# Differential attention's steps placed between the tiles of its input projection, modulation folds moved to the norms' waits, and tables for the square root fetched ahead

## The reference, cut to what matters

```python
q_x, k_x, v_x, gu_x, gv_x = jnp.split(hx @ w_in, AB_SPLITS, axis=-1)   # 4096 -> 8 chunks of 512
k_c, v_c = jnp.split(hc @ w_in[:, QK_W:2 * QK_W + V_W], [QK_W], axis=-1)
...
s = jnp.einsum('bqhmd,bkhmd->bhmqk', q, k) * ATTN_SCALE      # 8 heads, m = 2, 512 keys
p = jax.nn.softmax(s, axis=-1)
a = p[:, :, 0] - lam * p[:, :, 1]
o = jnp.einsum('bhqk,bkhe->bqhe', a, v)
...
y_x = jnp.concatenate([a_x, g_x], axis=-1) @ w_out
```

## Time and profile before

| | |
|---|---|
| Median of 3 runs | 2482.37 us (2480.27 to 2483.12) |
| The profiled execution | 2483.58 us; its span 2482.2 us |
| Mean granted TensorE clock | 0.961 of full speed |
| Busy | TensorE 2334.6 us (94%), VectorE 1830.6 (74%), ScalarE 1108.0 (45%), GpSimd 365.8 (15%) |
| 0 to 200 us | first block's attention |
| 190 to 390.7 us | up and down projection; of 245 to 290, TensorE is busy 45.00 |
| 400.4 to 546 us | second block's input projection; of 440 to 546, TensorE is busy 106.00 |
| 546 to 627 us | differential attention; of 571 to 608, TensorE is busy 28.00 |
| 633 to 668 us | output projection |
| 679 to 1541 us | first expert stage |

### The profile page before, as it was taken

One profiled execution on the slowest core, in us unless ns is written; L12 is line 12 of the kernel. 1 busy time (PEld: TensorE's weight loads), 2 busy tenths in 40 slices (PEclk: granted clock), 3 DMA queues, 4 the chain that ended last, 5 costly groups with the idle time before them and its releaser, 6 DMA issues.

```text
span 2482.2 us, 38990 instructions
## 1 busy us (share of the span) xinstructions
PE 2334.6 (94%) x15710; PEld 2059.9 (83%) x15710; DVE 1830.6 (74%) x3241; ACT 1108.0 (45%) x1571; POOL 365.8 (15%) x157
## 2 busy tenths in 40 slices
PE   7989998997899999999999997889999999999997
PEld 6769986774689999998777776779999999777785
DVE  8568988737538877778888876846986777888655
ACT  4446534325444444444444443444444444444443
POOL 0000004630434440000000000623440000000000
PEclk9779999998899999999999998989999999999998
DMA  8326674330245555555557884444555555556663
GB/s 295 122 85 210 205 292 176 125 105 1 94 170 179 180 178 165 168 171 170 170 170 276 306 331 172 165 163 157 171 182 166 166 167 169 171 171 218 222 213 118
DMA packets 123202, 442.58 MB, mean 178 GB/s; under 512 B 13696, under 2 KB 16768, under 8 KB 122256
## 3 DMA queue, kind: packets, MB, share of 16 engines
q1 hardware_dynamic: 117288, 425.04, 50.2%
q10 hardware_dynamic: 5736, 15.06, 1.8%
HBM read 436.88 MB, written 3.16 MB: 177 GB/s over the span
## 4 chain that ended last, share of the span: by engine, by line
PE 82%; DVE 13%; ACT 3%; issue 2%; DMA 0%; POOL 0%; ACTq 0%; SPq 0%; DVEq 0%
PE ps L377 25%; PE ps L378 25%; PE ps L379 25%; PE ps L2294 3%; DVE spl L2099 2%; DVE hT L1434 2%; ACT spl L934 1%; DVE acc L1454 1%; DVE hT L1432 1%; PE ps L406 1%; DVE xr L1950 1%; DVE xr L1955 1%; PE ps L2242 1%; ACT ex L1249 1%; DVE ex L1865 0%
## 5 line engine op out<-in xcount | busy, mean ns | idle before, releaser
L2099 DVE TENSOR_TENSOR spl<-ring,spl 128x1024 fp32r<-128x1024 f32 x561 | 691.0, 1233 | 400.6 <-ACT spl L934 399.3
L934 ACT ACTIVATE spl<-ring 128x1024 fp32r<-128x1024 f32 x703 | 738.2, 1052 | 497.2 <-PE ps L379 477.2
L377 PE MATMUL ps<-hT,spl 128*128 128x256 f32 x2656 | 765.4, 288 | 10.5 <-DVE spl L2099 8.5
L378 PE MATMUL ps<-hT,spl 128*128 128x256 f32 x2656 | 756.8, 285 | 0.0
L379 PE MATMUL ps<-hT,spl 128*128 128x256 f32 x2656 | 756.5, 285 | 0.0
L377 PEld LDWEIGHTS ps<-hT,spl 128*128 128x128 f32 x2656 | 515.1, 194 | 15.1 <-DVE spl L2099 9.3
L2355 POOL TENSOR_TENSOR spl<-ring,spl 128x1024 fp32r<-128x1024 f32 x142 | 353.6, 2497 | 1109.4 <-ACT spl L934 1109.3
L378 PEld LDWEIGHTS ps<-hT,spl 128*128 128x128 f32 x2656 | 515.7, 194 | 0.0
L379 PEld LDWEIGHTS ps<-hT,spl 128*128 128x128 f32 x2656 | 515.1, 194 | 0.0
L377 PE MATMUL ps<-spl,Ws 128*128 128x512 f32 x1024 | 414.4, 405 | 10.8 <-DVE Ws L2107 10.6
L378 PE MATMUL ps<-spl,Ws 128*128 128x512 f32 x1024 | 406.9, 397 | 0.0
(11 more groups left out here) (374 smaller groups left out, 2502.6 us busy)
## 6 DMA issues: line engine op xcount, KB each, us to landing
ring<-in_peer_u SPq DMA_DIRECT2D x256, 512.0 KB, 3.5
ring<-in_peer_v SPq DMA_DIRECT2D x256, 512.0 KB, 3.5
vring<-in_ada_w SPq DMA_DIRECT2D x56, 512.0 KB, 6.2
ring<-in_w_up SPq DMA_DIRECT2D x44, 512.0 KB, 4.3
aring<-in_ada_w SPq DMA_DIRECT2D x40, 512.0 KB, 5.5
ring<-in_ab_in SPq DMA_DIRECT2D x32, 512.0 KB, 3.4
ring<-in_peer_wq SPq DMA_DIRECT2D x32, 512.0 KB, 3.9
ring<-in_w_down SPq DMA_DIRECT2D x22, 512.0 KB, 5.3
```

The source lines that it names most:

```text
L377: q.matmul(o, l[0], r[0], start=start, stop=False)
L378: q.matmul(o, l[0], r[1], start=False, stop=False)
L934: q.activation(P.spl[:, m % SPLITS, 0, 0:w], P.ring[:, m % SLOTS, 0:w], ACT.Copy).then_inc(*P.hi.mark(m))
L2099: q.tensor_tensor(P.spl[:, n % SPLITS, 1, 0:w], P.ring[:, n % SLOTS, 0:w], P.spl[:, n % SPLITS, 0, 0:w].bitcast(F32), ALU.subtract).then_i ...
```

## The change

- **Attention between tiles.** The chunks now come in the order 2, 0, 4, 3, 1, 5, 7, 6. The transposes of queries and keys and the steps are called from within the tile loop, on all three engines: steps 0 to 9 behind the ten tiles from chunk 3's first on, steps 10 to 17 behind the eight tiles of chunks 7 and 6, steps 18 and 19 in the output stage. `ab_step(s)` says which head-half is scored, transposed and multiplied in a step. Steps have one pair of score banks and one bank each for transposes and values, no longer two. The rotations, the gate's norm and lambda are likewise called at single tiles.
- **Low halves** of all tiles before the first expert stage are VectorE's (`lo_on_dve`).
- **Context.** Its modulation goes from VectorE in the projection to ScalarE (two passes) and VectorE (one) at every second down tile.
- **Folds.** 0 goes behind the output projection of the first block, 3 and 4 behind the down projection, 9 and 10 behind the first expert stage, each between the last tile and `pe_turns`. The three modulation steps in the first output projection go to the up projection. Folds no longer all wait for the one before, only for one that shares a bank.
- **Up projection.** The cast of the product goes to ScalarE, and the split trails one pair of tiles.
- **Tables.** A one-column square root (`act_ready_sqrt`) at seven places loads the table ahead.
- **Output stage.** The groups come in the order 0, 1, 4, 5, 2, 3 and are copied and split in pairs of 512 columns; four output tiles run before heads 4 to 7 are transposed.

```diff
+AB_CHUNK = (2, 0, 4, 3, 1, 5, 7, 6)
+AB_STEP = {(3 + s // 4, s % 4): s for s in range(10)}
+AB_STEP.update({(6 + s // 4, s % 4): 10 + s for s in range(8)})
+AB_TURN = {(1, 3): ("KTc", 0), (2, 0): ("KT", 0), (2, 2): ("QT", 0), (5, 2): ("KTc", 1), (5, 3): ("KT", 1),
+           (6, 0): ("QT", 1)}
+def ab_step(s):
+    first, s = 8 * (s // 10), s % 10
+    return (first + s if s < 8 else None, first + s - 1 if 1 <= s < 9 else None, first + s - 2 if s >= 2 else None)
...
-    folds = [("ret", 7), ("up", 42), ("dn", 9), ("dn", 17), ("ab", 6)]
-    folds += [("v", 0, places[8 * i + 7][2] + 3) for i in range(5, 11)] + [("v", 1, 84)]
+    folds = [("wo_end",), ("up", 42), ("dn", 9), ("dn_end",), ("dn_end",)]
+    folds += [("v", 0, places[8 * i + 7][2] + 3) for i in range(5, 9)] + [("v_end",), ("v_end",), ("v", 1, 84)]
...
-    return n < T_AB
+    return n < T_PEER[0]
...
+def act_ready_sqrt(q, P, i):
+    q.wait_ge(*P.set_dve.at("eps"))
+    q.activation(P.none[:, i:i + 1], P.eps1[:, 0:1], ACT.Sqrt).then_inc(*P.line("none").mark())
...
 def pe_ab(q, P):
...
-            pe_fold(q, P, ("ab", 4 * i + p))
+            if (i, p) in AB_TURN:
+                pe_diff_turn(q, P, *AB_TURN[i, p])
+            if (i, p) in AB_STEP:
+                pe_diff_step(q, P, AB_STEP[i, p])
...
+def pe_diff_step(q, P, s):
...
+        for m in range(2):
+            if n % 8:
+                q.wait_ge(*act.at(("x", n - 1, m)))
+            q.matmul(P.ps[4 + m][:, :], P.QT[64 * m:64 * m + 64, h, tb * 128:(tb + 1) * 128],
+                     P.KT[64 * m:64 * m + 64, h, :], start=True, stop=True).then_inc(*pe.mark(("s", n, m)))
+    if nt is not None:
+        q.wait_ge(*dve.at(("mixed", nt)))
...
+        for j in range(4):
+            t = q.transpose(P.ps[6][:, j * 128:(j + 1) * 128], P.ex(nt, 0)[:, j * 128:(j + 1) * 128], P.ident[:, :])
...
 def act_ab(q, P):
...
         for p in range(4):
             act_hi(q, P, T_AB + 4 * i + p + 2)
...
+            if (i, p) in AB_STEP:
+                act_diff_step(q, P, AB_STEP[i, p])
...
 def dve_ab(q, P):
...
         for p in range(4):
-            dve_ada(q, P, ("ab", 4 * i + p))
+            if p == 0 and i and AB_BANK[i - 1][1]:
+                evz(i - 1)
+            dve_lo(q, P, T_AB + 4 * i + p + 2)
...
+            if (i, p) in ropes:
+                rope(*ropes[i, p])
...
+            elif i == 7 and p in (0, 2):
+                dve_gate_norm(q, P, p, act, dve)
...
+            if (i, p) in AB_STEP:
+                dve_diff_step(q, P, AB_STEP[i, p])
...
+def dve_diff_step(q, P, s):
...
+        q.wait_ge(*act.at(("x", nt, 1)))
+        q.reciprocal(z, z).then_inc(*dve.mark())
...
+    if n is not None:
+        for m in range(2):
+            q.wait_ge(*pe.at(("s", n, m)))
+            q.tensor_reduce(P.nm[:, 2 * n + m:2 * n + m + 1], P.ps[4 + m][:, :], AX, ALU.max, negate=True).then_inc(
+                *dve.mark(("mx", n, m)))
...
 def dve_pool(q, P):
...
-    dve_folds(q, P, dve, (1, 0), (1, 1))
+    dve_folds(q, P, dve, (1, 0))
+    dve_ada(q, P, ("v_end",))
+    dve_folds(q, P, dve, (1, 1))
```

More of the change, by code:

```diff
@@ L683, in pe_down @@
         pe_fold(q, P, ("dn", k))
-AB_CHUNK = [(i + 6) % 8 for i in range(8)]
+    pe_fold(q, P, ("dn_end",))
 def pe_ab(q, P):
@@ new lines, in pe_abo, with turns, tile @@
+def pe_abo(q, P):
+    bpe, bact, bdve = P.stage("ab")
+    dpe, dact, ddve = P.stage("da")
+    pe, act, dve = P.stage("abo")
+    def turns(g, bank, free):
+        q.wait_ge(*free)
+        for k in (2 * g, 2 * g + 1):
+            for tb in range(2):
+                q.wait_ge(*(ddve.at(("head", tb, k // 4 * 4)) if k < 8 else bdve.at(("gated", tb))))
+                o = k % 2 * 256 + tb * 128
+                t = q.transpose(P.ps[bank][:, o:o + 128], P.MB[:, tb, k * 128:(k + 1) * 128], P.ident[:, :])
+        t.then_inc(*pe.mark(("turn", g)))
+    def tile(c, j):
+        n = T_ABO + 6 * c + j
+        sl = pe_take(q, P, n)
+        for ks in range(2):
+            k = 2 * ABO_TILE[j] + ks
+            if c == 0:
+                q.wait_ge(*dve.at(("lo", k // 2)))
+            for tb in range(2):
+                if k == 0 and tb == 0:
+                    q.wait_ge(*dact.at(("x", 15, c)))
+                elif k == 0:
+                    q.wait_ge(*(ddve.at(("ao", 15)) if c else dact.at(("eT", 15))))
+                t = mm3(q, P.ps[4 + c + 2 * tb][:, :],
+                        cut(both(P.MT), lambda v: v[:, k, tb * 128:(tb + 1) * 128]),
+                        cut(sl, lambda v: v[:, ks * 512:(ks + 1) * 512]), k == 0, k == 7)
+                if ks == 1:
+                    t.then_inc(*pe.mark(("k", c, k, tb), *([("used", n)] if tb else []),
+                                        *([("y", tb, c)] if k == 7 else [])))
@@ L851, in pe_pool @@
+        t.then_inc(*P.line("ab_pe").mark(("gate", tb)))
+    for g in range(2):
+        turns(g, 2 + g, bact.at(("ev", 7, g)))
+    pe_diff_step(q, P, 18)
+    for g in range(2):
+        turns(4 + g, g, bdve.at(("gated", g)))
+    pe_diff_step(q, P, 19)
+    for j in range(4):
+        tile(0, j)
+    for g in range(2):
+        turns(2 + g, 2 + g, act.at(("turn", g)))
+    for j in range(4, 6):
+        tile(0, j)
+    for j in range(6):
+        tile(1, j)
 def pe_pool(q, P):
@@ new lines, in act_ab @@
+            name, hf = AB_TURN.get((i, p), ("KTc", 0))
+            if name != "KTc":
+                dst, b = (P.KT[:, :, 256:512], 6) if name == "KT" else (P.QT, 4)
+                if name == "KT" and hf == 0:
+                    q.wait_ge(*P.ada_pe.at(("fold", ADA_FRONT - 1)))
+                for g in (2 * hf, 2 * hf + 1):
+                    q.wait_ge(*dpe.at((name, g)))
+                    q.activation(dst[:, 2 * g:2 * g + 2, :], P.ps[b + g % 2][:, :].rearrange("p (k t) -> p k t", k=2),
+                                 ACT.Copy).then_inc(*dact.mark((name, g)))
@@ L1314, in act_peer @@
     tmp = P.ln[key][3][:, :].rearrange("p (a n) -> p a n", a=4)
-    q.wait_ge(*before[2].at("folds"))
+    q.wait_ge(*before[2].at(("folds", l, 1)))
     act_turned(q, pe, act, P.ps, tmp, P.adc[:, l, 3, :], P.adc[:, l, 2, :])
@@ new lines, in dve_head_ms, with dve_head_rms @@
+def dve_head_ms(q, P, h0):
+    act, dve = P.stage("da")[1:]
+    w, x = (v.rearrange("p (t h) -> p t h", t=2)[:, :, h0:h0 + 4] for v in (P.hr, P.hs))
+    q.wait_ge(*act.at(("hs", 2 * h0 + 7)))
+    q.tensor_scalar(w, x, 1.0 / 128, LN_EPS, ALU.mult, ALU.add).then_inc(*dve.mark(("hms", h0)))
+def dve_head_rms(q, P, h0):
+    act, dve = P.stage("da")[1:]
+    hr = P.hr.rearrange("p (t h) -> p t h", t=2)[:, :, h0:h0 + 4]
+    q.wait_ge(*act.at(("hsd", h0)))
+    q.reciprocal(hr, hr).then_inc(*dve.mark())
@@ L1931, in dve_abo, with parts @@
 def dve_abo(q, P):
-    bdve = P.stage("ab")[2]
+    bpe, bact, bdve = P.stage("ab")
     pe, act, dve = P.stage("abo")
+    def parts(*groups):
+        for g in groups:
+            x = P.tmpm[:, (0, 1, 4, 5, 2, 3).index(g) % 2, :].rearrange("p (k t) -> p k t", k=2)
+            hi, lo = P.MT[:, 0, 2 * g:2 * g + 2, :], P.MT[:, 1, 2 * g:2 * g + 2, :]
+            q.wait_ge(*act.at(("turn", g)))
+            q.tensor_copy(hi, x).then_inc(*dve.mark())
+            q.wait_ge(*dve.now())
+            q.tensor_tensor(lo, x, hi.bitcast(F32), ALU.subtract).then_inc(*dve.mark(("lo", g)))
+    q.tensor_scalar(P.dg, P.wcol("dng"), 1.0 - LAM_INIT, None, ALU.mult).then_inc(*dve.mark("dg"))
+    for tb in range(2):
+        q.wait_ge(*bpe.at(("gate", tb)))
+        q.wait_ge(*bact.at(("ev", 7, tb)))
+        for g in range(4):
+            q.scalar_tensor_tensor(
+                out=P.MB[:, tb, 1024 + g * 128:1152 + g * 128], in0=P.ps[tb][:, g * 128:(g + 1) * 128],
+                scalar=P.wcol("sgb", g), in1=P.U[:, tb, g * 128:(g + 1) * 128], op0=ALU.add,
+                op1=ALU.mult).then_inc(*bdve.mark(*([("gated", tb)] if g == 3 else [])))
+    dve_diff_step(q, P, 18)
+    parts(0, 1)
+    dve_lo(q, P, T_ABO + 2)
+    parts(4, 5)
+    dve_diff_step(q, P, 19)
+    dve_head_ms(q, P, 4)
+    dve_lo(q, P, T_ABO + 3)
+    dve_head_rms(q, P, 4)
+    dve_lo(q, P, T_ABO + 5)
+    parts(2, 3)
+    for n in range(6, 14):
+        dve_lo(q, P, T_ABO + n)
     dve_folds(q, P, dve, (0, 1))
-    q.tensor_scalar(P.dg, P.wcol("dng"), 1.0 - LAM_INIT, None, ALU.mult).then_inc(*dve.mark("dg"))
-    for k in range(12):
-        q.wait_ge(*act.at(("turn", k)))
-        hilo(q, dve, P.MT, k, P.tmpm[:, k // 2 % 2, k % 2 * 256:k % 2 * 256 + 256], ("lo", k))
     dve_ln(q, P, "abo", pe, act, dve)
@@ L2215, in pe_peer @@
     if l == 0:
-        first = [b4act.at(("turn", k)) for k in (9, 11, 5, 7)]
+        first = [b4act.at(("turn", g)) for g in (4, 5, 2, 3)]
     else:
@@ L2324, in pe_program @@
     pe_ab(q, P)
-    pe_diff(q, P)
     pe_abo(q, P)
```

641 lines of the change are left out of this document (297 added, 344 removed).

## The result

The changed kernel takes 2459.55 us (median of four runs, 2458.06 to 2464.22), the kernel before beside it 2481.32 (2477.16 to 2483.12): a ratio of 0.9918, 95% interval 0.9899 to 0.9937. The profiled run of the changed kernel took 2458.46, its span is 2456.8 against 2482.2. The forecast was 2457 between 2438 and 2476. The total is right; a sum of terms can be right by luck, so the stretches are compared one by one.

A forecast was written before the change was run, and what follows sets the result against it. TensorE, with 82% of the chain, was taken to bound the kernel. Gains of 4.0, 2.4, 1.9, 6.5 and 11 make 25.8 us; 2483.6 less that and 1.2 for the median gives 2457, range 2438 to 2476.

The forecast's parts named there:

- Fold 0: Between retention and the next transposes: without its 32 one-column matmuls there, 4.0 us gained, bounds 0 and 6.8.
- Norm after the output projection: First block: earlier residual add and early square-root table, less 0.4 for the fold moved in, gain 2.4 us, bounds 1 and 3.
- Up projection: Three double steps in on VectorE, 22 casts to ScalarE: no cost, hidden by TensorE; up to 1 us if not.
- Norm after the down projection: Fold 3 moved into the gap and the table load gone, less 1.3 us of lateness: gain 1.9, bounds 0.5 and 3.
- Projection and attention: Second block's projection and differential attention, steps woven between tiles: 10.5 us less 4 for clock, gain 6.5, bounds -10 and 27.
- The loop of 7.1 us: Woven attention steps behind small tiles: VectorE's and ScalarE's queue orders close a loop of 7.1 us a step.
- the loop is not closed: Rival, woven attention steps: halves run in the queues' slack, TensorE alone sets each step at 5.6 us; 2430 us, chance 0.10.
- The clock: Woven projection and attention: long waits lower TensorE's granted clock, 4 us taken off the gain, between 0 and 12.
- Folds 9 and 10: End of the first expert stage, moved into the norm's gap: 5.0 + 7.3 - 1.0, gain 11 us, bounds 7 and 12.5.
- the table switch costs its drain: Rival, ScalarE's table loads: each switch costs a drain besides the load; 2463 us, chance 0.03.
- The weave gives nothing: Rival, projection and attention: twelve loops each about 1 us longer, clock takes its 12; 2464 to 2472 us, chance 0.22.
- the clock falls and stays: Rival, woven attention steps: at half clock twelve loops need up to 11.2 us each; 2502 us, slower than before, chance 0.08.

The follow-up runs named there:

- steps_and_fold0_back: The changed kernel with fold 0 back in the retention stage and three double modulation steps back in the first output projection: 2462.5 us, 2.9 more.
- the opened kernel: The changed kernel with VectorE's low half of a projection tile behind the attention step's mix instead of ahead of it: 2436.5 us, 23.0 less.

## Why the prediction was right, and where only its sum was

That the total came out within 3 us is in part luck. The 8.5 us lost in the up projection were nearly made good by 6.5 us in five terms that were too small, part of them scatter and clock, and by 1.5 us at the start that no edit made.

- **Fold 0**: 4.0 said, 4.2 measured, by the mechanism named: the third group of transposes waits 2.41 us for ScalarE, and that is what is left of the 6.8.
- **Norm after the output projection**: 2.4 said, 3.4 measured (2.5 of it from fold and steps, as `steps_and_fold0_back` shows, 0.9 from the table). I had counted the table at 1.28 and fold 0 at 0.4 of new length. The fold takes 3.65 and TensorE is ready just as the normed rows are, so it cost nothing. The gap went from 6.36 to 3.75 us: 0.9 by the table, and 1.7 because VectorE now adds the residual 0.2 us before TensorE's end and not 1.5 us behind it.
- **Up projection**: the step that failed. "Nothing, hidden by TensorE's matmuls; if that cover failed it would cost up to 1 us" was written from a timeline in which TensorE showed no gap. That says that VectorE kept up, not by how much. The sum that was missing is VectorE's own pair: 5.21 and five steps made 5.76 of TensorE's 5.86, 22 x 0.1 = 2.2 us of slack for 7.2 us of steps. The 22 casts taken off would have paid for them, with the eviction first (5.82). But the cast was looked at as work and not as a place in ScalarE's order, ahead of the eviction for which VectorE waits. The bound of 1 us had no row behind it; the stage lost 8.5.
- **Norm after the down projection**: 1.9 said, 3.2 measured, 3.1 against the mean of ten. Fold 3's 1.84 are there. The table gave 0.9 and not 1.28, and the lateness of 1.3 came as 1.0: VectorE adds the residual 0.9 us behind TensorE's last projection matmul (387.55 against 386.66), and 0.1 us ahead of it before (390.56 against 390.7). The two cancel in the gap. What the forecast did not have is 1.5 in the projection itself, about what its higher clock in the first 14 us comes to.
- **Projection and attention**: 6.5 said, 8.2 measured in this trace, 7.1 against the mean of six. The loop of 7.1 us is shown by three experiments that change it in different places (23.0, 6.6 and 12.3 us less). In the forecast it was only a term of the cost; it was not asked what the same model says of another order. The rival "the loop is not closed" (2430, though its own 29 off 2457 give 2428) is what the kernel comes near when the loop is opened: 2435.
- **The clock**: 4 us were taken off. Windows with long waits had 0.88 and 0.93 (0.76 for the like in the earlier trace rows), the opened kernel 1.00 and 0.92. The direction is right; how much of the 23 us is clock was not measured apart.
- **Folds 9 and 10**: 11 said; undoing them cost 11.3 in the stretch and 9.1 to 10.4 in the medians. 1.6 of fold 10's wait was VectorE's low half beside GpSimd, which the forecast counted in the 3.46 without naming it. The late column sums, 1.0 said, are 0.81.

Of the rivals, "the table switch costs its drain" is out by 1.30 us from load to root. "The weave gives nothing" and "the clock falls and stays" did not happen. The first was costed too low: 12 us for the loops and 12 for the clock against a gain of 10.5 make 13.5 us above and not 8, so about 2477 and not 2472.

## What to carry to other kernels

A stage in which TensorE has no gap is no free cover: take one period of the loop, add up what each other engine does and waits for in it, and compare that with TensorE's period before putting anything in. When work goes to another engine, look at what stands behind it in that engine's queue and who waits for that; a short cast that waits for an engine makes that engine wait for all that stands behind the cast. When a loop over two or three queues sets the pace, write down its terms and ask of each whether it must be in the loop: here one pass moved behind another was worth as much as the whole change.

## What the runs showed of the hardware

GpSimd beside VectorE slowed VectorE's passes over memory (0.42 to 2.62, 1.22 to 2.85, and a mean of 0.97 instead of 0.49 us), not the reductions from the accumulators (0.68). Yet with the low halves' subtraction on GpSimd the kernel was 12 us faster, since the engines worked side by side. TensorE's values took 1.06 us at full clock behind a wait of 2.16 us, 1.43 behind one of 2.46, and 1.92, at the lower of the two levels, behind waits of 3.69 and 3.74, as at 501.50 above. The length of the wait alone does not tell the level: behind a wait of 1.92 us they took 1.06 in the changed kernel and 1.92 with the cast back on VectorE, and behind one of 3.73 they took 1.06 with the eviction first and 1.92 with the high half behind the exponentials. And a table load on ScalarE started ahead of the wait of the instruction that needed it, so a late load cost 0.9 us at each of the two norms and not its 1.28.
